# Attention's value product turned round: values as a split stationary operand, one key-value group per unit

## The reference, cut to what matters

```python
qg = q.reshape(B, Q, N_KV_HEADS, Q_PER_KV, HEAD_DIM).astype(jnp.float32)
logits = jnp.einsum('bqngd,bqknd->bqngk', qg, kg.astype(jnp.float32)) * (HEAD_DIM ** -0.5)
logits = jnp.where(valid[:, :, None, None, :], logits, NEG)
p = jax.nn.softmax(logits, axis=-1)
o = jnp.einsum('bqngk,bqknd->bqngd', p, vg.astype(jnp.float32))
```

## Time and profile before

| | us |
|---|---|
| median of 3 runs | 3634.23 (3627.4 to 3640.02) |
| the profiled execution's own time | 3627.5 |
| its span | 3625.8 |
| PE busy | 3036.5 (84%) |
| PE weight loads | 2396.8 (66%) |
| DVE busy | 1840.4 (51%) |
| ACT busy | 1637.7 (45%) |
| POOL busy | 1262.6 (35%) |
| mean granted TensorE clock | 0.915 of 2.4 GHz |

### The profile page before, as it was taken

The page is one execution under the profiler, slowest core; times in us unless marked ns, Lnnn a source line. Parts: engine busy times, 40 slices in busy tenths (PEclk is TensorE's granted clock), DMA queues, the critical chain, the costliest instruction groups (busy, mean ns, idle before and its releaser), DMA issues.

```text
span 3625.8 us, 46903 instructions
## 1 busy us (share of the span) xinstructions
PE 3036.5 (84%) x15347; PEld 2396.8 (66%) x15352; DVE 1840.4 (51%) x4116; ACT 1637.7 (45%) x2873; POOL 1262.6 (35%) x1181
## 2 busy tenths in 40 slices
PE   7998545546678889997799999968989999699997
PEld 5887431224556668764577886645778888588885
DVE  4433872862357884468686332666782333511112
ACT  3322413612447755575463555745634554322222
POOL 1333621324013561153265113522672112224444
PEclk9999777877879999998899999988999999899999
DMA  4444344636336564354454223343444213544443
GB/s 149 142 146 142 93 126 133 170 118 202 111 123 232 206 244 134 115 200 154 157 193 169 79 85 124 126 171 122 177 159 136 73 62 131 191 147 150 174 151 125
DMA packets 216109, 529.45 MB, mean 146 GB/s; under 512 B 57514, under 2 KB 110828, under 8 KB 189852
## 3 DMA queue, kind: packets, MB, share of 16 engines
q1 hardware_dynamic: 202924, 501.94, 40.6%
q0 software_dynamic: 11360, 22.60, 2.0%
q10 hardware_dynamic: 1584, 1.90, 0.2%
HBM read 399.43 MB, written 134.12 MB: 147 GB/s over the span
## 4 chain that ended last, share of the span: by engine, by line
PE 50%; DVE 11%; issue 9%; ACT 5%; DMA 4%; POOL 4%; SPq 2%; ACTq 0%; POOLq 0%; DVEq 0%
PE r L1620 16%; PE r L1657 12%; PE po L1708 6%; PE tr L1699 3%; ACT junk_a_b L1982 2%; PE sc L1686 2%; PE sc L1687 2%; POOL acc_b L2124 1%; PE sc L1676 1%; DVE junk_v_b L2363 1%; PE r L1817 1%; POOL hr_b L2105 1%; DVE trial_b L2315 1%; PE tr L1676 1%; PE r L1586 1%
## 5 line engine op out<-in xcount | busy, mean ns | idle before, releaser
L2124 POOL TENSOR_TENSOR acc_b<-acc_b,part_b 128x512 f32<-128x512 f32 x375 | 516.2, 1398 | 483.0 <-ACT part_b L1933 482.1
L1657 PE MATMUL r<-ready_b,h_b 128*128 128x512 f32 x2304 | 574.4, 403 | 41.5 <-ACT part_b L1933 38.3
L1657 PEld LDWEIGHTS r<-ready_b,h_b 128*128 128x128 f32 x2304 | 434.2, 193 | 155.5 <-ACT part_b L1933 51.1
L1620 PE MATMUL r<-x_hi_b,ready_b 128*128 128x512 f32 x1536 | 516.5, 400 | 5.4 <-DVE x_lo_b L2229 2.8
L2105 POOL TENSOR_TENSOR hr_b<-hr_b 128x512 f32<-128x512 f32 x128 | 149.0, 1164 | 766.7 <-ACT hr_b L1920 766.5
L1982 ACT ACTIVATE junk_a_b<-score_b,trial_b 128x384 int8<-128x384 f32 (+13 forms) x266 | 347.4, 1306 | 100.8 <-DVE trial_b L2315 99.7
L1620 PEld LDWEIGHTS r<-x_hi_b,ready_b 128*128 128x128 f32 x1536 | 291.3, 190 | 72.2 <-issue 10.1
L1933 ACT ACTIVATE part_b<-r 128x512 f32<-128x512 f32 x390 | 223.9, 595 | 220.5 <-PE r L1657 131.8
L1708 PEld LDWEIGHTS po<-V_sb,pT_b 128*128 128x128 f32 x2176 | 286.7, 191 | 23.4 <-ACT pT_b L2009 4.5
L1620 PE MATMUL r<-x_lo_b,ready_b 128*128 128x512 f32 x768 | 301.6, 393 | 0.0
L1708 PE MATMUL po<-V_sb,pT_b 128*128 128x64 f32 x2176 | 279.2, 268 | 3.7 <-DVE o_b L2380 3.3
(11 more groups left out here) (407 smaller groups left out, 6061.1 us busy)
## 6 DMA issues: line engine op xcount, KB each, us to landing
ready_b<-ws_u SPq DMA_DIRECT2D x96, 1024.0 KB, 6.6
ready_b<-ws_d SPq DMA_DIRECT2D x96, 1024.0 KB, 5.0
ws_u<-up_b SPq DMA_DIRECT2D x32, 1024.0 KB, 8.7
ws_d<-dn_b SPq DMA_DIRECT2D x30, 1024.0 KB, 6.4
kv_b<-kv_pages POOLq DMA_DIRECT2D x128, 128.0 KB, 3.5
kv_b<-kv_pages SPq DMA_DIRECT2D x128, 128.0 KB, 3.1
raw_b<-w_out SPq DMA_DIRECT2D x64, 256.0 KB, 3.2
raw_b<-w_up SPq DMA_DIRECT2D x32, 512.0 KB, 5.4
```

The source lines that it names most:

```text
L1620: mm = pe.matmul(x[:], wt[:, c], y[:, k], start=k == n == 0, stop=(k, n) == (KD - 1, 2))
L1657: mm = pe.matmul(x[:], f[:, tok], w[:, col], start=c == n == 0, stop=(c, n) == (KQ - 1, 2))
L2124: pool.tensor_tensor(dst, dst, part[:, add_no[key] % 2, :], ALU.add).then_inc(add_pool, 1)
```

## The change: what it does

Values are now kept as a high (fp32r) and a low part side by side, 2 x 64 columns, and stand in PE as weights (`V2[:, k, :]`). The probabilities' transposed tile is also split into high and low, 2 x 128 columns, and moves past. One fp32r matmul of 256 columns per key tile gives four blocks in one PSUM bank; rows are value dimensions (high, then low), columns are queries (high, then low). So per head DVE adds the two column halves (`sum_values`), and PE adds the two row halves and turns the block back to queries by 64 in one fp32 matmul with a stacked identity (`fold_values`). DVE then scales each head (`output`), 128 times, where before it scaled 16 tiles.

The probabilities' way is now: ACT copies `tr` to `raw_pT`; DVE rounds it to the high part (`high_prob`); POOL subtracts for the low part (`low_prob`). `values` waits for POOL. `turn_output` handles 2 blocks per tile and group where it handled 4 per tile.

Attention is cut by key-value group: eight units (`LOTS`), each one stage and one group, with its own AB (cost 4.0) and A steps (cost 0.45). A unit has `ahead` = banks + 1 lead steps (as many as before in the stages with feed) and 7 tail steps (before 6). `KS` and `V2` hold one group and are reloaded for each unit up to the stage's width, and mask tiles are loaded once per group. `mk` gets a place of its own; the two masks that POOL makes itself are stored to DRAM for the second group. `project_inputs` stores the split values per tile. A wait on the sample keys' load is moved to its users, and some load semaphores are merged.

```diff
-                    dve.tensor_copy(R["V"][:, t, :], pr[:, s, OFF_V:OFF_QI])
+                    v = pr[:, s, OFF_V:OFF_QI].rearrange("p (v d) -> p v d", d=HD)
+                    if t >= 2:
+                        dve.wait_ge(out_ok[s], 160 * (t // 2))
+                    dve.tensor_copy(v2[:, s, :, 0], v).then_inc(v_hi_ok, 1)
                     dve.wait_ge(pr_ok, 4 * t + 3)
-                    dve.tensor_copy(R["wi"][:, t, :], pr[:, s, OFF_WI:OFF_U]).then_inc(copied, 1)
+                    dve.tensor_copy(R["wi"][:, t, :], pr[:, s, OFF_WI:OFF_U])
+                    dve.wait_ge(v_hi_ok, t + 1)
+                    dve.tensor_tensor(v2[:, s, :, 1], v, v2[:, s, :, 0].bitcast(F32), ALU.subtract).then_inc(copied, 1)
                     dve.wait_ge(ropeq, 4 * t + 3)
...
-    n_bank = lambda s: 4 * NH * (s + 1)
-    ahead = lambda s: s + 2
+    LOTS = tuple((ts, v) for ts in ATTEND for v in range(NKV))
+    n_bank = lambda s: 4 * QPK * banks(LOTS[s][0][0])
+    ahead = lambda s: banks(LOTS[s][0][0]) + 1
+    STEPS = 7
 
     def attend_units(s):
-        return [(("AB", s), 8.0)] + [(("A", s, j), 0.5) for j in range(-ahead(s), n_bank(s) + 6)]
+        return [(("AB", s), 4.0)] + [(("A", s, j), 0.45) for j in range(-ahead(s), n_bank(s) + STEPS)]
...
+                def load_keys_of(s):
+                    ts, v = LOTS[s]
+                    n = width(ts[-1])
+                    if s:
+                        sp.wait_ge(sc_full, first_score(s))
+                    for z, name in enumerate(("kh_d", "kl_d")):
+                        sp.dma_start(KS[HD * z:HD * z + HD, 0:n].bitcast(F32), A[name][HD * v:HD * v + HD, 0:n]).then_inc(ks_ld, 16)
+
+                def load_values_of(s):
+                    ts, v = LOTS[s]
+                    if s:
+                        sp.wait_ge(pT_used, first_score(s))
+                    sp.dma_start(V2[:, 0:ts[-1] + 1].bitcast(F32), A["v2_d"][v, :, 0:ts[-1] + 1].rearrange("p t z d -> p t (z d)")).then_inc(v2_ld, 16)
...
+                    if j + ahead(s) == n_bank(s) + 1 and s + 1 < len(LOTS):
+                        load_keys_of(s + 1)
+                    if j == n_bank(s) + 3 and s + 1 < len(LOTS):
+                        load_values_of(s + 1)
...
                 def values(t, h, b):
-                    pe.wait_ge(tr_free, turn_no["p", t, h, b] + 1)
-                    if h == b == 0 and t:
-                        pe.wait_ge(o_ok, t)
-                    n = HD * (h // QPK)
+                    n = head_no[t, h]
+                    pe.wait_ge(pT_lo_ok, prob_no[t, h, b] + 1)
+                    if b == 0:
+                        wait(pe, vsum_ok, n)
+                        if h % QPK == 0:
+                            pe.wait_ge(v2_ld, 16 * (LOTS.index((ATTEND[t // 4], h // QPK)) + 1))
                     for k in range(4 * b, min(4 * b + 4, t + 1)):
-                        mm = pe.matmul(po[:, h, :], pT[:, prob_no[t, h, b] % 3, k - 4 * b, :], R["V"][:, k, n:n + HD],
+                        mm = pe.matmul(po[:, 0, :], V2[:, k, :], pT[:, prob_no[t, h, b] % 3, k - 4 * b].rearrange("p z q -> p (z q)"),
                                        start=k == 0, stop=k == t)
                     mm.then_inc(pT_used, 1)
 
-                def turn_output(t):
-                    pe.wait_ge(o_ok, t + 1)
-                    x = turn_bank(("o", t))
-                    for f in range(4):
-                        mm = pe.transpose(x[:, f * P:(f + 1) * P], o[:, 2 * f:2 * f + 2, :].rearrange("p h d -> p (h d)"), ident[:])
+                def fold_values(t, h):
+                    n = head_no[t, h]
+                    pe.wait_ge(vsum_ok, n + 1)
+                    if n == 0:
+                        pe.wait_ge(mz_ok, 4)
+                    x = turn_bank(("f", t, h))
+                    pe.matmul(x[:, 0:HD], vsum[:], halves_one[:], start=True, stop=True).then_inc(tr_full, 1)
+
+                def turn_output(t, v):
+                    i = item_no[t, v]
+                    pe.wait_ge(o_ok, head_no[t, QPK * v + QPK - 1] + 1)
+                    x = turn_bank(("o", t, v))
+                    for f in range(2):
+                        mm = pe.transpose(x[:, f * P:(f + 1) * P], o[:, i % 2, 2 * f:2 * f + 2, :].rearrange("p h d -> p (h d)"), ident[:])
                     mm.then_inc(tr_full, 1)
...
                     if (s, j + ahead(s)) in bank_of:
                         scores(*bank_of[s, j + ahead(s)])
+                    if head_end(s, j - 3):
+                        fold_values(*head_end(s, j - 3))
                     if (s, j - 2) in bank_of:
                         values(*bank_of[s, j - 2])
-                    if tile_at(s, j - 4) is not None:
-                        turn_output(tile_at(s, j - 4))
+                    if (s, j - 5) in item_at:
+                        turn_output(*item_at[s, j - 5])
...
                 def keep_prob(t, h, b):
                     i, j = turn_no["p", t, h, b], prob_no[t, h, b]
-                    wait(act, pT_used, j - 2)
                     m = min(4, t + 1 - 4 * b)
                     act.wait_ge(tr_full, i + 1)
-                    act.activation(pT[:, j % 3, 0:m, :], tr[i % 2][:, 0:m * P].rearrange("p (k q) -> p k q", q=P),
-                                   ACT.Copy).then_inc(tr_free, 1)
+                    wait(act, pT_lo_ok, j - 1)
+                    act.activation(raw_pT[:, j % 2, 0:m], tr[i % 2][:, 0:m * P].rearrange("p (k q) -> p k q", q=P),
+                                   ACT.Copy).then_inc(pT_raw_ok, 1)
 
...
+                def low_prob(t, h, b):
+                    j, m = prob_no[t, h, b], min(4, t + 1 - 4 * b)
+                    hi, lo = pT[:, j % 3, 0:m, 0, :].bitcast(F32), pT[:, j % 3, 0:m, 1, :]
+                    pool.wait_ge(pT_hi_ok, j + 1)
+                    pool.tensor_tensor(lo, raw_pT[:, j % 2, 0:m], hi, ALU.subtract).then_inc(pT_lo_ok, 1)
...
-                def output(t):
-                    dve.wait_ge(prob_ok, head_no[t, NH - 1] + 1)
-                    c.step(dve.reciprocal(rinv[:], rsum[:, t % 2, :]))
-                    dve.wait_ge(pT_used, prob_no[t, NH - 1, banks(t) - 1] + 1)
-                    if t:
-                        dve.wait_ge(tr_full, turn_no["o", t - 1] + 1)
-                    dve.tensor_tensor(o[:], po[:], rinv[:, :, None].to_broadcast([P, NH, HD]), ALU.mult).then_inc(o_ok, 1)
+                def high_prob(t, h, b):
+                    j, m = prob_no[t, h, b], min(4, t + 1 - 4 * b)
+                    dve.wait_ge(pT_raw_ok, j + 1)
+                    wait(dve, pT_used, j - 2)
+                    dve.tensor_copy(pT[:, j % 3, 0:m, 0, :], raw_pT[:, j % 2, 0:m]).then_inc(pT_hi_ok, 1)
+
+                def sum_values(t, h):
+                    n = head_no[t, h]
+                    dve.wait_ge(pT_used, prob_no[t, h, banks(t) - 1] + 1)
+                    if n:
+                        dve.wait_ge(tr_full, turn_no["f", *head_at[n - 1]] + 1)
+                    c.step(dve.tensor_copy(vsum[:], po[:, 0, 0:P]))
+                    dve.tensor_tensor(vsum[:], po[:, 0, P:2 * P], vsum[:], ALU.add).then_inc(vsum_ok, 1)
+
+                def output(t, h):
+                    n, a, i = head_no[t, h], h % QPK, item_no[t, h // QPK]
+                    c.step(dve.reciprocal(rinv[:, a:a + 1], rsum[:, i % 2, a:a + 1]))
+                    dve.wait_ge(tr_full, turn_no["f", t, h] + 1)
+                    if a == 0 and i >= 2:
+                        dve.wait_ge(tr_full, turn_no["o", *items[i - 2]] + 1)
+                    x = tr[turn_no["f", t, h] % 2]
+                    dve.tensor_scalar(o[:, i % 2, a, :], x[:, 0:HD], rinv[:, a:a + 1], None, ALU.mult).then_inc(o_ok, 1)
 
...
+                    if (s, j - 1) in bank_of:
+                        high_prob(*bank_of[s, j - 1])
                     if (s, j + ahead(s)) in bank_of:
                         mask_scores(*bank_of[s, j + ahead(s)])
-                    if tile_at(s, j - 2) is not None:
-                        output(tile_at(s, j - 2))
+                    if head_end(s, j - 3):
+                        output(*head_end(s, j - 3))
+                    if head_end(s, j - 2):
+                        sum_values(*head_end(s, j - 2))
 
```

245 lines of the change are left out of this document (143 added, 102 removed).

## The result

The changed kernel takes 3737.94 us (median of 3 runs, 3727.03 to 3742.0) against 3634.23: a ratio of 1.0285, 95% interval 1.026 to 1.0311. The profiled execution has a span of 3736.3 us. The forecast was 3595, its range ended at 3685.

What follows compares the result with a forecast made beforehand. PE was taken to bound stages 1 to 3. Stage terms -27, -22, -10, +10, seams +8 and projection +2 sum to -39 against the profiled 3627.5, giving 3588.5, or 3595 at the runs' median; range 3530 to 3685.

Steps and rivals of the forecast that it cites:

- 8 records, four key tiles, hold PE from 2859.33 to 2860.34, 0.2525 us a tile: Old value product in attention: PE's cost per key tile, read from the timeline as 0.2525 us.
- 1088 x 0.135 = 146.9 us go: Value product: 1088 matmuls, each falling from 0.2525 to 0.1175 us, save PE 146.9 us before the folds.
- the forecast 114.6: Attention, PE: net gain of 114.6 us, after 32.3 for 128 folds; by stage 2.7, 20.0, 37.3, 54.5.
- the first rival: Attention stages: PE's whole gain arrives, DVE and POOL fit between; -102 us, 3532 us; chance 0.20.
- Demand on what both need: Stage 3: DVE and POOL cannot overlap, so their work adds up to 250 us against PE's 239.
- The 15 of stage 3: Stage 3: POOL idles in 29 feed instructions until an ACT copy of about 0.6 us ends, half exposed: 15 us.
- +10, -10, -22, -27: Attention stages 0 to 3: forecast changes in length, in us, against the kernel before.
- 0 to 6 us at each of the four new seams; I take 2: +8: Unit changes within stages: reloading keys and values costs 2 us at each of four seams, +8 us.
- `project_inputs` ... about 0.3 x 17 = 5 us beside PE ... +2 (0 to +8): Projection: one more DVE subtraction a tile, 5 us beside PE, and one more store; +2 us, 0 to +8.
- my own rule on the two engines: Attention: GpSimd and DVE's two-port modes share a port pair, locked per instruction, so `high_prob` cannot run beside `low_prob`.
- DVE copies whose median lies well above 0.44 us: Sign expected in the trace after: DVE's copies stretch beside POOL, their median well above 0.44 us.
- Rival 3: Attention: ACT, DVE and POOL in series set the step; +73 us, 3707 us; chance 0.20.

Runs made afterwards that it cites:

- overlapping units: Changed kernel with values split late, early queries, one value sum, and a first unit's tail steps interleaved with the second's lead: 3666.0 us, 1.01 of the kernel before.
- units_alone: Changed kernel with the value product of the kernel before, units and the projection's extra work kept: 3710.0 us, 1.0215 of the kernel before.
- late_v2: Changed kernel with the projection's two DVE instructions on values moved behind the low parts, and their store behind the next loads: 3717.4 us, 1.0243 of the kernel before.

## Why the prediction was wrong

By the runs the changed kernel's loss is 20 us for the projection, 60 for the cut into units and 28 for the new product. The forecast had +2, +8 and, in its sum by stage, -49. The miss is therefore 18, 52 and 77 us, and the largest part is the gain that PE was to bring.

- **"8 records, four key tiles, hold PE from 2859.33 to 2860.34, 0.2525 us a tile" and "1088 x 0.135 = 146.9 us go": wrong, and the step that carried the rest.** The earlier trace rows are weight loads, which run beside matmuls, and 0.1175 was read from matmuls. By matmuls the old product took 0.2025 a tile, and the new one has a median of 0.55 us for a full bank. From the start of a matmul to the next one's, less idle time, the value matmuls of the whole kernel fall from 225.9 to 154.3 us and the folds add 28.7: a net gain of 42.9 us, and 45.0 by busy time in the overlapping units, for the forecast 114.6. With it PE's demand in stage 3 is 264 us and not 239, above the 250 that was taken as the bound, and even the first rival gives 3601 and not 3532. The number of records and GpSimd's work came as forecast (1088, +351 us), DVE's +253 for 290.
- **"Demand on what both need" (250 against PE's 239): wrong in kind.** I added up busy times of engines that pass a bank on, and allowed 15 to 20 us a stage for waits. (The 15 of stage 3 is also not what its sentence says: half of 29 x 0.6 is 9.) GpSimd's work costs 41 us in the changed kernel and 32 in the overlapping units, though its busy share is 43% of the span and 64% of the last stage there: that did not mean that it was hidden. With the seams overlapped, where the comparison is cleanest, the stages are +15.2, +9.1, +3.0 and -11.3 us against before, for a forecast of +10, -10, -22, -27. Without GpSimd's work they are +12.8, +3.7, -7.7 and -23.2. The last is PE's whole gain there and near the forecast, but for a reason that the forecast didn't have; it had expected PE's 54 less waits for GpSimd. These windows hold 12, 2 and -12 feed matmuls more than before in stages 1 to 3, some 3 us at most.
- **"0 to 6 us at each of the four new seams; I take 2: +8": wrong by 52 us.** I priced the landing of 1 MB and not the order of SP's queue, nor that a seam is lead and tail of a pipeline in which PE has little to do. The cut costs 60 us (units_alone less the projection). Early queries and interleaving give 27 back (interleaving alone 30 in the kernel with the new product), and 23 of what is left fall in search stages that I had said the change doesn't touch.
- **"`project_inputs` ... about 0.3 x 17 = 5 us beside PE ... +2 (0 to +8)": wrong.** The subtraction cost 0.98 and the copy 0.53 a tile beside GpSimd's rotation, and they were not beside PE but ahead of the low parts on which SP's loads wait. Measured 20.5. The 0.3 is what the subtraction takes clear of GpSimd (0.29 in late_v2); my own rule on the two engines was applied to attention only.
- **"DVE copies whose median lies well above 0.44 us": wrong.** The median is 0.42; only the mean of full banks, 0.571, is above, and the same copies without GpSimd's low parts have 0.495. The lock is there all the same: of 224 full copies 72 begin inside a low part and 129 beside nothing of GpSimd. The sign asked for a median where a third of the copies meet the subtraction.
- **Rival 3 named the side but not the mechanism:** it put 19 us on stages 2 and 3 each by steps in series (11 measured in each, seams and more feed work included), 15 on stage 0 (25, most of it work from outside), 10 on the seams. Its 3707 was 31 us short, for the projection and the search stages, and as near as it was by luck: it too built on PE's 0.1175.

From the kernel before to the changed one, by the runs: projection 20.5, early loads and value sum 21.7, overlap of the units 29.7, GpSimd's low parts 32.0; what then is left is 4 us, in which the cut's remaining cost of some 33 stands against PE's gain. The terms were taken off in this order, and the 21.7 holds some 5 of scatter.

## What to carry to other kernels

Take the cost of an operation before and after from the same kind of row: a weight load's row beside a matmul's overstated the gain here more than twofold, and a cut that costs 60 us can't be paid from 45. A change that needs memory may be paid for with a cut of the work into units; price the cut first, by what PE has to do between a unit's last and the next one's first instruction, and by what stands ahead of the new loads in the queue that issues them. Before an operation is called hidden, ask where it stands in its engine's order and who waits for the instruction behind it: the same work cost 20 us in one place of the projection and nothing that shows in another. When three engines hand on a bank, their busy shares don't add up to a bound; take the work of one of them out in a run to see its price.

## What was not expected of the hardware

A DVE subtraction of 128 columns took 977 to 995 ns in all 17 tiles beside GpSimd, and 0.29 us where it met none of its arithmetic. A DVE copy that began inside a GpSimd subtraction ended 0.28 us after it, and an addition of a broadcast zero 0.55 us after it, whenever they had begun; alone the two took 0.42 and 0.68 us for 512 columns. GpSimd's own instruction had a mean of 1289 and 1288 ns for 512 columns in both kernels. And PE's granted clock did not follow the idle share of the last stage: 0.96 with an idle share of 11%, 1.00 with 9% when the units overlap, 0.99 with 1% before the change.
